# One float per run: a broadcast skip vector loaded in place, and the small loads of the start put under one semaphore

## The chip, the cores and the metric

The kernel runs on 1 core of one Trainium2 chip. The metric is the device time of one execution in microseconds (us), as the median of several executions. The time before is 993.97 us, the median of three (991.53 to 995.42).

## What is computed

Two layers of a decoder trunk on 256 tokens of width 1024, all in float32. Layer 0 mixes with a pooling group and a Mamba-2 group, layer 1 with a Conformer convolution and a gated short convolution. Every layer then cross-attends into 256 memory tokens and applies a squared-ReLU MLP. Cut to what the change touches:

```
h   = rmsnorm(x, g[0]);  u = h @ w_in                     # layer 0: ab_w_in, 1024 x 3088
pool_u, z, xbc, dt_raw = split(u)
pool_out = (window_mean(pool_u) - pool_u) @ pool_w[g]     # four groups; pool_w is 4 x 128 x 128
xbc = silu(causal_dwconv(xbc, conv_w) + conv_b)
dt  = softplus(dt_raw + dt_bias);  a = -exp(a_log)        # 16 heads
y   = ssd_chunked(xs, dt, a, B, C) + d_skip[head] * xs    # d_skip: 16 floats, one for each head of 64 channels
x   = x + rmsnorm(concat(pool_out, gated_norm(y)) @ w_out, g[1])
x   = x + rmsnorm(cross_attn(rmsnorm(x, g[2]), mem, ...), g[3])   # mem: 256 x 1024
x   = x + rmsnorm(mlp(rmsnorm(x, g[4])), g[5])
```

## The kernel before

Activations are kept transposed: a tile has channels on the 128 partitions and the 256 tokens along the row, so 1024 channels are eight such tiles (`J` = 8). To keep float32 precision every matmul operand is split into a rounded high part and a low part, and a product is three matmuls: high x high, high weight x low activation, low weight x high activation (`three`, L496 to L498).

**Weights come in units.** A unit is 256 rows x 512 columns (512 KB), two tiles of 128 rows. `weight_plan` lists 284 of them in the order in which they are used. SyncE issues one DMA for each into one of six slots of `raw` (L469). ScalarE rounds it into `w_hi` (L919). VectorE (L1263) or GpSimd (L1891) subtracts to make `w_lo`. TensorE then runs 24 matmuls on it (two tiles x four column blocks x three). From unit 6 on the DMA waits until TensorE has finished the unit that held the slot.

**Each engine's order is written out by hand**, and an engine does its instructions in that order. SyncE at the start: `x` into `xtok`, units 0 to 3, then `later_inputs` (eleven small loads into `stage`, `wdt` and the vectors), units 4 and 5, then `mem_inputs` (L459 `poolw`, L460 `memtok`), and then unit 6, the first that waits. `wdt` is the 16 columns of `ab_w_in` that give dt; `dtb`, `expA` and `dall` are 16-float vectors repeated on all 128 partitions.

**ScalarE at the start**: for each of the eight h tiles, `round_to(j // 2 + 1)` and then the scaled high part `h_hi` (L937). So h tiles 6 and 7 stand behind the rounding of unit 4. After them come the two sums of squares (L948), the copy of the norm factor's row into `Rrow` (L951), `expA` (L954), unit 5 (L919) and the copy of the vectors (L965).

**VectorE at the start**: the low parts `h_lo` (L1274), `w_lo` of unit 4, the mean square (L1295), a wait for four loads on `ssm_landed`, two copies (L1300) that pick the even and the odd heads out of `dall` for the lower and the upper 64 partitions of `dskip`, eight small multiplies that make `wdtg` (L1303), and then the first projected tiles (L1309), which need `Rrow`. The depthwise convolution (L1329, L1332) follows.

**GpSimd** makes the norm factor from the mean square by a power (L1914), and TensorE spreads it into a row after unit 3 (L577, the matmuls that `Rrow` copies). TensorE needs h tile 6 for the first matmul of unit 3, waits for `poolw` only after the SSD part, and for `memtok` after the second group of projections.

`dskip` is read once, in `gate_y`, as a per-partition scalar.

Of the kernel before, what the change touches and what calls it, by code (L numbers as in the profile page):

```python
# [38 lines left out]
P = 128  # L39
SLOTS = 6  # L40
# [4 lines left out]
class Ledger:  # L45
# [5 lines left out]
    def tick(self, sem, *label):  # L51
        self.count[sem] = self.count.get(sem, 0) + 1
        if label:
            assert (sem, *label) not in self.at, label
            self.at[(sem, *label)] = self.count[sem]
        return 1

    def after(self, sem, *label):
        if self.known is None:
            return 1  # L60
        return self.known[(sem, *label)]
# [168 lines left out]
def trunk(nc, A, out, known):  # L230
    T = A["x"].shape[1]
    D = A["x"].shape[2]
    J = D // P
    HEADS = A["ssm_a_log"].shape[1]
# [4 lines left out]
    tick, after, now = L.tick, L.after, L.now  # L239
# [39 lines left out]
    with ctx:  # L279
        def sb(name, shape, dt=F32, scope=ctx):  # L280
            return scope.enter_context(nc.sbuf_tensor(name, [P, *shape], dt))

        def sem(name):
            return ctx.enter_context(nc.semaphore(name))
# [31 lines left out]
        with ExitStack() as s:  # L316
            xdt = sb("xdt", [TT, D], scope=s)
            mp_hi, mp_lo = sb("mp_hi", [4, T], F32R, s), sb("mp_lo", [4, T], F32R, s)
            E = sb("E", [4, 3 * P], scope=s)
            cbm = sb("cbm", [2, 3 * P], scope=s)  # L320
            zs = sb("zs", [J, T], scope=s)
            xc = sb("xc", [12, T], scope=s)
            upad = sb("upad", [2, 2, T + 3], scope=s)
            pu = sb("pu", [4, T + 16], scope=s)
            pw1, pw2 = sb("pw1", [T + 16], scope=s), sb("pw2", [T + 16], scope=s)
            pdiff = sb("pdiff", [4, T], scope=s)
            Sg = sb("Sg", [2, T], scope=s)
            Rg = sb("Rg", [2, T], scope=s)
            icnt = sb("icnt", [4, 16], scope=s)
            poolw = sb("poolw", [4, P], scope=s)  # L330
            wdt, wdtg = sb("wdt", [J, HEADS], scope=s), sb("wdtg", [J, HEADS], scope=s)
            dtT = sb("dtT", [T], scope=s)
            dtb, expA, dskip = sb("dtb", [HEADS], scope=s), sb("expA", [HEADS], scope=s), sb("dskip", [J], scope=s)
            dall = sb("dall", [HEADS], scope=s)
            sp = sb("sp", [10, 2 * HEADS], scope=s)
            cs = sb("cs", [4, HEADS], scope=s)
        with ExitStack() as s:
# [11 lines left out]
        with ExitStack() as s:  # L349
# [4 lines left out]
        ps = ctx.enter_context(nc.psum_tensor("ps", [P, 8, 512], F32))  # L354


        x_landed, gain_landed, mem_landed, vec_landed, ssm_landed, poolw_landed, out_stored = (
            sem(n) for n in ("x_landed", "gain_landed", "mem_landed", "vec_landed", "ssm_landed", "poolw_landed",
                             "out_stored"))
        raw_landed = [sem(f"raw_landed{i}") for i in range(SLOTS)]  # L360
        hi_ready, lo_ready_dve, lo_ready_pool = (sem(n) for n in ("hi_ready", "lo_ready_dve", "lo_ready_pool"))

        pe_made, act_made, dve_made, pool_made = sem("pe_made"), sem("act_made"), sem("dve_made"), sem("pool_made")
# [15 lines left out]
        misc_at, n = {}, 0  # L379
# [17 lines left out]
        def bank2(label):  # L397
            return ps[:, use[label][0], :].rearrange("p (c t) -> p c t", c=2)

        def full(label):  # L400
            return pe_made, after("pe", label)

        def freed(engine, label):
            L.at[("free", label)] = (engine, now(engine))
# [37 lines left out]
        @block.sync  # L442
        def _(sp_):
            sp_.dma_start(xtok[:, :, :], A["x"][0].rearrange("(t p) d -> p t d", p=P)).then_inc(x_landed, 16)

            def later_inputs():
                for name, v in MISC_ROWS:
                    r0 = misc_at[name] - MISC
                    sp_.dma_start(stage[r0:r0 + v.shape[0], 1, :], v).then_inc(vec_landed, 16)
                sp_.dma_start(stage[:, 2, :], dw_rows[0:P, :]).then_inc(vec_landed, 16)  # L450
                sp_.dma_start(stage[0:DWN - P, 3, :], dw_rows[P:DWN, :]).then_inc(vec_landed, 16)
                sp_.dma_start(wdt[:, :, :], A["ab_w_in"][0, :, 3072:3088].rearrange("(j p) h -> p j h", p=P))\
                    .then_inc(ssm_landed, 16)
                sp_.dma_start(dtb[:, :], A["ssm_dt_bias"].broadcast_to([P, HEADS])).then_inc(ssm_landed, 16)
                sp_.dma_start(expA[:, :], A["ssm_a_log"].broadcast_to([P, HEADS])).then_inc(ssm_landed, 16)
                sp_.dma_start(dall[:, :], A["ssm_d"].broadcast_to([P, HEADS])).then_inc(ssm_landed, 16)

            def mem_inputs():
                sp_.dma_start(poolw[:, :, :], A["pool_w"][0].rearrange("g i o -> i g o")).then_inc(poolw_landed, 16)  # L459
                sp_.dma_start(memtok[:, :, :], A["mem"][0].rearrange("(t p) d -> p t d", p=P)).then_inc(mem_landed, 16)  # L460

            for u in range(NU):
                if u == 4:
                    later_inputs()
                if u == SLOTS:
                    mem_inputs()
                if u >= SLOTS:
                    sp_.wait_ge(pe_made, after("pe", "unit", u - SLOTS))
                sp_.dma_start(raw[:, u % SLOTS, :, :], units[u]).then_inc(raw_landed[u % SLOTS], 16)  # L469
            for i in range(4):  # L470
                hf, t = i // 2, i % 2
                sp_.wait_ge(dve_made, after("dve", "otok", i))
                sp_.dma_start(out[0, t * P:(t + 1) * P, hf * 512:(hf + 1) * 512],
                              otok[:, t, hf * 512:(hf + 1) * 512]).then_inc(out_stored, 16)
            sp_.wait_ge(out_stored, 16 * 2 * TT)
# [3 lines left out]
        def _(pe):  # L479
# [189 lines left out]
            for i in range(8):  # L669
                g = i // 4  # L670
# [13 lines left out]
                if i >= 2:  # L684
                    y_pair(i - 2)

            pe.wait_ge(poolw_landed, 16)
            for i in range(2):
                acquire(("pooled", i))
                for c in range(2):  # L690
                    g = 2 * i + c
# [219 lines left out]
        def _(act):  # L911
# [38 lines left out]
            act.wait_ge(*full(("R0",)))  # L950
            nc.scalar.activation(Rrow[:, :], bank(("R0",))[:, 0:T], ACT.Copy).then_inc(act_made, tick("act", "Rrow", 0))  # L951
            freed("act", ("R0",))
            act.wait_ge(ssm_landed, 16 * 4)
            nc.scalar.activation(expA[:, :], expA[:, :], ACT.Exp).then_inc(act_made, tick("act", "expA"))  # L954

            def silu_pair(i):
# [76 lines left out]
            for i in range(2):  # L1033
                for c in range(2):
                    g = 2 * i + c
# [80 lines left out]
            for l in range(2):  # L1116
                m_out = [("out", l, g, q) for g in range(2) for q in range(2)]
                if l == 1:
# [14 lines left out]
                    for g in range(2):  # L1133
                        for q in range(2):
                            i = 2 * g + q
# [101 lines left out]
            for g in range(2):  # L1237
# [6 lines left out]
                for i in (2 * g, 2 * g + 1):  # L1244
                    for c in range(2):
                        j = 2 * i + c
# [6 lines left out]
        def _(dve):  # L1253
            V = nc.vector
# [12 lines left out]
            def own():  # L1267
                dve.wait_ge(dve_made, now("dve"))
# [24 lines left out]
            for t in range(TT):  # L1293
                dve.wait_ge(act_made, after("act", "ss0", t))
            V.tensor_scalar(stat[:, 1, 0:2], stat[:, 0, 0:2], 1.0 / D, RMS_EPS, ALU.mult, ALU.add)\  # L1295
                .then_inc(dve_made, tick("dve", "v0"))
            dve.wait_ge(ssm_landed, 16 * 4)
            dpair = dall[:, :].rearrange("p (j two) -> p j two", two=2)
            for hf in range(2):
                V.tensor_copy(dskip[64 * hf:64 * hf + 64, :], dpair[64 * hf:64 * hf + 64, :, hf])\  # L1300
                    .then_inc(dve_made, tick("dve", *(("dskip",) if hf else ())))
            for j in range(J):
                V.tensor_scalar(wdtg[:, j, :], wdt[:, j, :], gain(0, 0, j), None, ALU.mult)\  # L1303
                    .then_inc(dve_made, tick("dve", *(("wdtg",) if j == J - 1 else ())))
# [134 lines left out]
            def gate_y(i):  # L1439

                dve.wait_ge(*full(("y", i)))
                dve.wait_ge(act_made, after("act", "z", i))
                dve.wait_ge(dve_made, after("dve", "dskip"))
                if i:
                    dve.wait_ge(dve_made, after("dve", "yg", i - 1))
                for c in range(2):
                    j = 2 * i + c
                    V.scalar_tensor_tensor(out=tmp[:, c, :], in0=xc[:, j, :], scalar=dskip[:, j:j + 1],
                                           in1=bank2(("y", i))[:, c, :], op0=ALU.mult, op1=ALU.add)\
                        .then_inc(dve_made, tick("dve"))  # L1450
                freed("dve", ("y", i))
                own()
                V.tensor_tensor(zs[:, 2 * i:2 * i + 2, :], zs[:, 2 * i:2 * i + 2, :], tmp[:, :, :], ALU.mult)\
                    .then_inc(dve_made, tick("dve", "yg", i))
# [36 lines left out]
            for g in range(4):  # L1491
# [4 lines left out]
                if g % 2 == 1:  # L1496
                    freed("dve", ("pooled", g // 2))
            gate_y(2)
            gate_y(3)
            group_sum(1)  # L1500
            low_to(F_[("out", 0, "early", 1)] + 3)
# [228 lines left out]
            for l in range(2):  # L1730
                if l == 1:
# [7 lines left out]
                    for g in range(2):  # L1739
# [9 lines left out]
                        for q in range(2):  # L1749
                            i = 2 * g + q  # L1750
# [9 lines left out]
                    for g in range(2):  # L1760
# [4 lines left out]
                        for q in range(2):  # L1765
                            i = 2 * g + q
# [5 lines left out]
                            for k in range(3):  # L1772
                                own()
                                for c in range(2):
                                    j = 2 * i + c
# [11 lines left out]
                    for g in range(2):  # L1787
                        for q in range(2):
                            i = 2 * g + q
# [81 lines left out]
            for i in range(4):  # L1871
                g, t = i // 2, i % 2
# [174 lines left out]
```

## Time and profile before

| | |
|---|---|
| median of three runs | 993.97 us (991.53 to 995.42) |
| the profiled execution | 995.42 us, of which its span is 993.5 us |
| TensorE matmul busy | 926.3 us (93%) |
| VectorE busy | 668.4 us (67%) |
| ScalarE busy | 472.1 us (48%) |
| GpSimd busy | 315.3 us (32%) |
| mean granted TensorE clock | 0.974 of full speed |
| DMA | 153.74 MB, 155 GB/s on average |

The rows further down are of the profiled execution. Times count from the start of its span, so a row "17.73 1.06" began at 17.73 us and was busy for 1.06 us. A bracket at the end of a row gives how long the engine had been idle just before it and what released it. A DMA's row on SPq is the time that SyncE took to issue it; when it landed is a separate column.

### The profile page before, as it was taken

The numbers are of one execution on the slowest core, as the hardware profiler recorded it, in microseconds if no ns is written. First come the engines' busy times: TensorE is split into PE (matmuls) and PEld (weight loads), VectorE is DVE, ScalarE is ACT, GpSimd is POOL, SyncE is SP. The second block draws the span as 40 slices with busy tenths as digits, with TensorE's granted clock in tenths as the row PEclk, the third lists the DMA queues.
The fourth block names the chain that finished last, engine by engine and source line by source line (L and its number), as shares of the span: only waits on it lengthen the run. The fifth ranks groups of instructions, "written<-read, shape, count | busy, mean of one in ns | idle before, by whom it ended". The sixth has DMA issues, their size and how long they took to land.

```text
span 993.5 us, 17155 instructions
## 1 busy us (share of the span) xinstructions
PE 926.3 (93%) x7268; PEld 899.3 (91%) x7268; DVE 668.4 (67%) x1013; ACT 472.1 (48%) x660; POOL 315.3 (32%) x213
## 2 busy tenths in 40 slices
PE   5978988989999999999989998999998889999997
PEld 5878987879898999999989998889998789999996
DVE  6796497686648655455588999986586385544553
ACT  4443444454546444444454433636465364444443
POOL 3242482542324100000158877536441330000000
PEclk8998999999999999999999999999999989999999
DMA  8443532455354555665555555335542435565551
GB/s 269 136 128 99 177 107 65 148 161 159 106 170 148 190 172 174 202 186 184 188 148 170 182 180 157 100 107 169 170 149 75 138 122 175 173 198 188 186 190 44
DMA packets 81031, 153.74 MB, mean 155 GB/s; under 512 B 6251, under 2 KB 7227, under 8 KB 80955
## 3 DMA queue, kind: packets, MB, share of 16 engines
q1 hardware_dynamic: 80843, 152.60, 48.7%
q8 instruction: 57, 0.93, 0.4%
q14 instruction: 19, 0.16, 0.1%
q10 hardware_dynamic: 112, 0.05, 0.0%
HBM read 151.58 MB, written 1.05 MB: 154 GB/s over the span
## 4 chain that ended last, share of the span: by engine, by line
PE 70%; DVE 20%; ACT 3%; issue 3%; POOL 2%; DMA 1%; DVEq 0%; POOLq 0%; ACTq 0%
PE ps L496 21%; PE ps L498 21%; PE ps L497 21%; DVE ps L1618 5%; DVE w_lo L1263 3%; DVE xc L1332 2%; POOL w_lo L1891 1%; PE ps L735 1%; PE ps L737 1%; PE ps L736 1%; ACT w_hi L919 1%; DVE xc L1329 1%; PE ps L563 1%; DVE E L1480 1%; DVE cv L1781 1%
## 5 line engine op out<-in xcount | busy, mean ns | idle before, releaser
L919 ACT ACTIVATE w_hi<-raw 128x1024 fp32r<-128x1024 f32 x284 | 296.9, 1055 | 282.4 <-DMA raw<-in_mlp_w 146.7
L496 PE MATMUL ps<-h_hi,w_hi 128*128 128x256 f32 x1280 | 370.8, 290 | 30.9 <-issue 12.9
L497 PE MATMUL ps<-h_lo,w_hi 128*128 128x256 f32 x1280 | 368.1, 288 | 0.0
L498 PE MATMUL ps<-h_hi,w_lo 128*128 128x256 f32 x1280 | 367.7, 287 | 0.0
L1263 DVE TENSOR_TENSOR w_lo<-raw,w_hi 128x1024 fp32r<-128x1024 f32 x192 | 250.5, 1324 | 136.8 <-ACT w_hi L919 136.6
L1891 POOL TENSOR_TENSOR w_lo<-raw,w_hi 128x1024 fp32r<-128x1024 f32 x92 | 229.6, 2510 | 188.4 <-ACT w_hi L919 188.4
L496 PEld LDWEIGHTS ps<-h_hi,w_hi 128*128 128x128 f32 x1280 | 251.7, 197 | 35.6 <-issue 21.5
L497 PEld LDWEIGHTS ps<-h_lo,w_hi 128*128 128x128 f32 x1280 | 251.9, 197 | 0.0
L498 PEld LDWEIGHTS ps<-h_hi,w_lo 128*128 128x128 f32 x1280 | 251.7, 197 | 0.0
L1914 POOL TENSOR_TENSOR rfac<-stat,mhalf 128x2 f32<-128x2 f32 (+1 forms) x14 | 16.5, 1181 | 428.0 <-DVE stat L1548 334.3
L498 PE MATMUL ps<-r_hi,w_lo 128*128 128x256 f32 x512 | 143.8, 281 | 0.0
L496 PE MATMUL ps<-r_hi,w_hi 128*128 128x256 f32 x512 | 143.6, 280 | 0.0
L497 PE MATMUL ps<-r_lo,w_hi 128*128 128x256 f32 x512 | 142.4, 278 | 0.0
L497 PEld LDWEIGHTS ps<-r_lo,w_hi 128*128 128x128 f32 x512 | 96.3, 188 | 0.0
L496 PEld LDWEIGHTS ps<-r_hi,w_hi 128*128 128x128 f32 x512 | 96.3, 188 | 0.0
L498 PEld LDWEIGHTS ps<-r_hi,w_lo 128*128 128x128 f32 x512 | 96.1, 188 | 0.0
L1618 DVE SCALAR_TENSOR_TENSOR ps<-vpad,vecs,ps 128x256 f32<-128x256 f32 x203 | 84.5, 481 | 1.0
L1713 DVE SCALAR_TENSOR_TENSOR rsq<-ps,relu 128x512 f32<-128x512 f32 x32 | 22.0, 687 | 55.3 <-ACT relu L1107 55.3
L496 PE MATMUL ps<-mh,w_hi 128*128 128x256 f32 x128 | 37.2, 291 | 1.8 <-DVE ml L1852 1.8
L1110 ACT ACTIVATE r_hi<-rsq 128x512 fp32r<-128x512 f32 x32 | 20.2, 633 | 36.7 <-DVE rsq L1713 36.7
L496 PE MATMUL ps<-mem_hi,w_hi 128*128 128x256 f32 x128 | 37.1, 290 | 0.0
L497 PE MATMUL ps<-ml,w_hi 128*128 128x256 f32 x128 | 36.6, 286 | 0.0
(247 smaller groups left out, 1322.7 us busy)
## 6 DMA issues: line engine op xcount, KB each, us to landing
raw<-in_mlp_w SPq DMA_DIRECT2D x128, 512.0 KB, 3.8
raw<-in_cd_w_in SPq DMA_DIRECT2D x40, 512.0 KB, 3.7
raw<-in_xa_wkv SPq DMA_DIRECT2D x32, 512.0 KB, 3.8
raw<-in_ab_w_in SPq DMA_DIRECT2D x24, 512.0 KB, 3.8
raw<-in_xa_wq SPq DMA_DIRECT2D x16, 512.0 KB, 3.9
raw<-in_xa_wo SPq DMA_DIRECT2D x16, 512.0 KB, 3.8
raw<-in_cd_w_out SPq DMA_DIRECT2D x16, 512.0 KB, 3.9
raw<-in_ab_w_out SPq DMA_DIRECT2D x12, 512.0 KB, 3.7
```

The source lines that it names most:

```text
L496: nc.tensor.matmul(dst, wt[0], x[0], start=start, stop=False, skip_group_check=True)
L497: nc.tensor.matmul(dst, wt[0], x[1], start=False, stop=False, skip_group_check=True)
L498: return nc.tensor.matmul(dst, wt[1], x[0], start=False, stop=stop, skip_group_check=True)
L563: mm = nc.tensor.transpose(bank(label)[:, c:c + k], src, ident[0:k, 0:k])
L919: nc.scalar.activation(w_hi[:, v % SLOTS, :, :], raw[:, v % SLOTS, :, :], ACT.Copy)\
L1110: nc.scalar.activation(r_hi[:, h % 2, 2 * q:2 * q + 2, :], rsq[:, q, :].rearrange("p (c t) -> p c t", c=2), ACT.Copy)\
L1263: V.tensor_tensor(w_lo[:, v % SLOTS, :, :], raw[:, v % SLOTS, :, :], f(w_hi[:, v % SLOTS, :, :]), ALU.subtract).then_inc(lo_ready_dve, 1)
L1332: V.scalar_tensor_tensor(out=xc[:, j, :], in0=src, scalar=vec("convw", k * 12 + j), in1=xc[:, j, :], op0=ALU.mult, op1=ALU.add)\
L1618: V.scalar_tensor_tensor(out=acc if k < 30 else cv[:, j, :], in0=src, scalar=tap(k, j), in1=acc, op0=ALU.mult, op1=ALU.add)\
L1713: V.scalar_tensor_tensor(out=rsq[:, q, :], in0=bank(("w1", l, h, q)), scalar=0.0, in1=relu[:, q, :], op0=ALU.max, op1=ALU.mult)\
L1891: G.tensor_tensor(w_lo[:, v % SLOTS, :, :], raw[:, v % SLOTS, :, :], f(w_hi[:, v % SLOTS, :, :]), ALU.subtract).then_inc(lo_ready_pool, 1)
L1914: G.tensor_tensor(dst, src, mhalf[:, 0:dst.shape[1]], ALU.pow).then_inc(pool_made, tick("pool", *name))
```

## The change

The vector `ssm_d` is no longer loaded as `dall` and rearranged by VectorE. Two DMAs write it into `dskip` directly, one for each half of the partitions. Each takes every second of the 16 floats, eight of them, and repeats them on 64 partitions. `poolw` and `memtok` move from behind unit 5 to the end of `later_inputs`, ahead of unit 4. `poolw` now counts on `ssm_landed`. Every wait on that semaphore (VectorE before `wdtg`, ScalarE before `expA`, TensorE before the pooled matmuls) is for all six loads. The semaphore `poolw_landed`, the tile `dall`, the two copies and a wait for them in `gate_y` go away.

```diff
@@ sync engine, later_inputs
-                sp_.dma_start(dall[:, :], A["ssm_d"].broadcast_to([P, HEADS])).then_inc(ssm_landed, 16)
-
-            def mem_inputs():
-                sp_.dma_start(poolw[:, :, :], A["pool_w"][0].rearrange("g i o -> i g o")).then_inc(poolw_landed, 16)
+                for hf in range(2):
+                    sp_.dma_start(dskip[64 * hf:64 * hf + 64, :],
+                                  A["ssm_d"].rearrange("a (j two) -> a two j", two=2)[:, hf, :].broadcast_to([64, J]),
+                                  allow_slow_non_contiguous=True).then_inc(ssm_landed, 16)
+                sp_.dma_start(poolw[:, :, :], A["pool_w"][0].rearrange("g i o -> i g o")).then_inc(ssm_landed, 16)
                 sp_.dma_start(memtok[:, :, :], A["mem"][0].rearrange("(t p) d -> p t d", p=P)).then_inc(mem_landed, 16)
             for u in range(NU):
                 if u == 4:
                     later_inputs()
-                if u == SLOTS:
-                    mem_inputs()
@@ tensor engine
-            pe.wait_ge(poolw_landed, 16)
+            pe.wait_ge(ssm_landed, 16 * 6)
@@ scalar engine
-            act.wait_ge(ssm_landed, 16 * 4)
+            act.wait_ge(ssm_landed, 16 * 6)
@@ vector engine
-            dve.wait_ge(ssm_landed, 16 * 4)
-            dpair = dall[:, :].rearrange("p (j two) -> p j two", two=2)
-            for hf in range(2):
-                V.tensor_copy(dskip[64 * hf:64 * hf + 64, :], dpair[64 * hf:64 * hf + 64, :, hf])\
-                    .then_inc(dve_made, tick("dve", *(("dskip",) if hf else ())))
+            dve.wait_ge(ssm_landed, 16 * 6)
@@ gate_y
-                dve.wait_ge(dve_made, after("dve", "dskip"))
```

On SyncE's queue, from `wdt` to the first unit that waits, before (a row names the line, the tile written, the tensor read and the shape):

```order
L452 DMA wdt<-in_ab_w_in 128x8x16
L454 DMA dtb<-in_ssm_dt_bias 128x16
L455 DMA expA<-in_ssm_a_log 128x16
L456 DMA dall<-in_ssm_d 128x16
L469 DMA raw<-in_ab_w_in 128x2x512 x2
L459 DMA poolw<-in_pool_w 128x4x128
L460 DMA memtok<-in_mem 128x2x1024
L469 DMA raw<-in_ab_w_in 128x2x512 [waits pe_made] x18
```

and the same stretch with the change (line numbers from here on are up to three lower above `gate_y`):

```order
L450 DMA wdt<-in_ab_w_in 128x8x16
L452 DMA dtb<-in_ssm_dt_bias 128x16
L453 DMA expA<-in_ssm_a_log 128x16
L455 DMA dskip<-in_ssm_d 64x8x1 x2
L458 DMA poolw<-in_pool_w 128x4x128
L459 DMA memtok<-in_mem 128x2x1024
L466 DMA raw<-in_ab_w_in 128x2x512 x2
L466 DMA raw<-in_ab_w_in 128x2x512 [waits pe_made] x18
```

Units 4 and 5 (the pair `x2`) now stand last of the loads that wait for nothing, behind one more small DMA, the pooling weights and the memory tokens.

On VectorE, around the end of the first projection, before:

```order
L1263 TENSOR_TENSOR w_lo<-raw,w_hi 128x1024 [waits hi_ready]
L1295 TENSOR_SCALAR stat<-stat 128x2 [waits act_made]
L1300 COPY dskip<-dall 64x8 [waits ssm_landed]
L1300 COPY dskip<-dall 64x8
L1303 TENSOR_SCALAR wdtg<-wdt,vecs 128x16 x8
L1309 TENSOR_TENSOR upad<-ps,Rrow 128x2x256 [waits pe_made,act_made]
```

and with the change:

```order
L1260 TENSOR_TENSOR w_lo<-raw,w_hi 128x1024 [waits hi_ready]
L1292 TENSOR_SCALAR stat<-stat 128x2 [waits act_made]
L1296 TENSOR_SCALAR wdtg<-wdt,vecs 128x16 [waits ssm_landed]
L1296 TENSOR_SCALAR wdtg<-wdt,vecs 128x16 x7
L1302 TENSOR_TENSOR upad<-ps,Rrow 128x2x256 [waits pe_made,act_made]
```

The two copies are gone, and the wait on the small loads sits on the first multiply of `wdtg`.

## Rows read from the trace of the kernel before

**Rows 1.** Page: busy time; then the chain that ended last, share by engine.
```profile
PE 926.3 (93%) x7268; PEld 899.3 (91%) x7268; DVE 668.4 (67%) x1013; ACT 472.1 (48%) x660; POOL 315.3 (32%) x213
...
PE 70%; DVE 20%; ACT 3%; issue 3%; POOL 2%; DMA 1%; DVEq 0%; POOLq 0%; ACTq 0%
```

**Rows 2.** The chain around 28 us: start, length, engine, tile, line.
```profile
27.97 0.12 PE ps L498
28.09 0.46 PE ps L577 x4
28.55 0.02 issue
28.57 0.38 ACT Rrow L951
28.95 0.10 ACT expA L954
29.06 0.94 ACT w_hi L919
30.00 0.44 ACT vecs L965 x2
30.44 0.03 issue
30.46 2.12 DVE xc L1329
```

**Rows 3.** SyncE's queue, timeline: issue start, issue time, line, transfer.
```profile
7.65 0.40 SPq L452 DMA_DIRECT2D wdt<-in_ab_w_in  x1
8.09 1.67 SPq L454 DMA_DIRECT2D dtb<-in_ssm_dt_bias  x1
9.81 0.55 SPq L455 DMA_DIRECT2D expA<-in_ssm_a_log  x1
10.40 0.63 SPq L456 DMA_DIRECT2D dall<-in_ssm_d  x1
11.07 0.94 SPq L469 DMA_DIRECT2D raw<-in_ab_w_in  x2
12.06 0.90 SPq L459 DMA_DIRECT2D poolw<-in_pool_w  x1
13.00 1.10 SPq L460 DMA_DIRECT2D memtok<-in_mem  x1
```

**Rows 4.** DMA issues, 0 to 80 us: size, us from issue to landing.
```profile
memtok<-in_mem SPq DMA_DIRECT2D x1, 1024.0 KB, 9.5
poolw<-in_pool_w SPq DMA_DIRECT2D x1, 256.0 KB, 7.9
...
wdt<-in_ab_w_in SPq DMA_DIRECT2D x1, 64.0 KB, 5.4
...
dtb<-in_ssm_dt_bias SPq DMA_DIRECT2D x1, 8.0 KB, 5.9
expA<-in_ssm_a_log SPq DMA_DIRECT2D x1, 8.0 KB, 5.7
dall<-in_ssm_d SPq DMA_DIRECT2D x1, 8.0 KB, 5.9
```

**Rows 5.** Units 4, 5 and 6, issued from 10 to 20 us: landing min/median/max.
```profile
DMA to landing us min/median/max: 4.3/6.6/7.6
```

**Rows 6.** DMA packets from 11 to 12 us, and from 13 to 15 us.
```profile
DMA packets 1268, 0.16 MB, mean 156 GB/s; under 512 B 1094, under 2 KB 1268, under 8 KB 1268
...
DMA packets 158, 0.01 MB, mean 5 GB/s; under 512 B 158, under 2 KB 158, under 8 KB 158
```

**Rows 7.** Stretches: PE, PEld, DVE, ACT, POOL busy (instructions), PEclk, DMA share, GB/s.
```profile
11.00:12.00 1.00, 0.00 (x0) 0.00 (x0) 1.00 (x1) 1.00 (x3) 1.00 (x1) 1.00 1.38 156
...
13.00:14.00 1.00, 0.00 (x0) 0.00 (x1) 1.00 (x3) 1.00 (x3) 0.54 (x1) 0.50 0.03 4
14.00:15.00 1.00, 0.97 (x4) 1.00 (x5) 1.00 (x1) 0.19 (x1) 1.00 (x1) 0.50 0.05 6
...
16.00:17.00 1.00, 1.00 (x7) 1.00 (x6) 1.00 (x3) 0.00 (x0) 0.11 (x1) 0.50 1.06 410
```

**Rows 8.** ScalarE, timeline: start, busy, line, operation, idle before.
```profile
17.73 1.06 ACT L919 ACTIVATE w_hi<-raw 128x1024 fp32r<-128x1024 f32 x1 [3.54 <-DMA raw<-in_ab_w_in]
18.69 0.89 ACT L937 ACTIVATE h_hi<-xT,vecs 128x256 fp32r<-128x256 f32 x2
```

**Rows 9.** VectorE, timeline, 18 to 29 us.
```profile
18.24 1.86 DVE L1274 SCALAR_TENSOR_TENSOR h_lo<-xT,vecs,h_hi 128x256 fp32r<-128x256 f32 x4
...
21.91 0.17 DVE L1295 TENSOR_SCALAR stat<-stat 128x2 f32<-128x2 f32 x1 [0.67 <-ACT sq L948]
21.99 0.39 DVE L1300 COPY dskip<-dall 64x8 f32<-64x8 f32 x2
22.41 1.47 DVE L1303 TENSOR_SCALAR wdtg<-wdt,vecs 128x16 f32<-128x16 f32 x8
28.99 1.29 DVE L1309 TENSOR_TENSOR upad<-ps,Rrow 128x512 f32<-128x512 f32 x2 [5.12 <-ACT Rrow L951]
```

**Rows 10.** GpSimd's power and TensorE's R0, timeline.
```profile
22.16 0.72 POOL L1914 TENSOR_TENSOR rfac<-stat,mhalf 128x2 f32<-128x2 f32 x1 [6.05 <-DVE dskip L1300]
...
27.93 0.60 PE L577 MATMUL ps<-ident,rfac 128*128 128x128 f32 x4
```

**Rows 11.** TensorE, timeline: its first projection matmul, and unit 3's first.
```profile
14.03 0.55 PE L496 MATMUL ps<-h_hi,w_hi 128*128 128x256 f32 x1 [4.51 <-DVE h_lo L1274]
...
25.05 0.28 PE L496 MATMUL ps<-h_hi,w_hi 128*128 128x256 f32 x1
```

**Rows 12.** The chain: one matmul's step near 16 us, and one near 22 us.
```profile
16.07 0.21 PE ps L498
...
21.97 0.12 PE ps L496
```

More of the change, by code:

```diff
@@ L333, in trunk @@
             dtb, expA, dskip = sb("dtb", [HEADS], scope=s), sb("expA", [HEADS], scope=s), sb("dskip", [J], scope=s)
-            dall = sb("dall", [HEADS], scope=s)
             sp = sb("sp", [10, 2 * HEADS], scope=s)
@@ L354, in trunk @@
         ps = ctx.enter_context(nc.psum_tensor("ps", [P, 8, 512], F32))
-        x_landed, gain_landed, mem_landed, vec_landed, ssm_landed, poolw_landed, out_stored = (
-            sem(n) for n in ("x_landed", "gain_landed", "mem_landed", "vec_landed", "ssm_landed", "poolw_landed",
-                             "out_stored"))
+        x_landed, gain_landed, mem_landed, vec_landed, ssm_landed, out_stored = (
+            sem(n) for n in ("x_landed", "gain_landed", "mem_landed", "vec_landed", "ssm_landed", "out_stored"))
         raw_landed = [sem(f"raw_landed{i}") for i in range(SLOTS)]
```

## The prediction

> **What bounds the kernel now.** The page first: TensorE is busy for 93% of the span and holds 70% of the chain that ended last [rows 1], so over the whole run the kernel is bound by TensorE. The change touches only the first 30 us, and there the chain decides. It runs through TensorE's first four weight units to the matmuls that spread the norm factor (28.09), then through the copy into Rrow, expA, unit 5's rounding and the copy of the vectors to VectorE's convolution at 30.46 [rows 2]. Whatever makes that passage late makes all behind it late, since the convolution needs Rrow and VectorE's stream from there is on the chain. So two questions count: what does the change put ahead of that passage, and how much slack does each thing ahead of it have?
>
> **What is removed.** Two copies of 0.39 us together [rows 9] and two waits. Behind them VectorE sits idle for 5.12 us until Rrow comes [rows 9], and GpSimd's power needs the mean square, which stands ahead of the copies. Taking the copies away is worth nothing. One small DMA (dall) goes too, and is priced below with what takes its place.
>
> **What is moved: poolw and memtok, ahead of units 4 and 5.** SyncE's queue gave its loads in the order wdt, dtb, expA, dall, unit 4, unit 5, poolw, memtok [rows 3]. From issue and time to landing [rows 3, 4], wdt landed at 7.65 + 5.4 = 13.05, dtb at 8.09 + 5.9 = 14.0, expA at 9.81 + 5.7 = 15.5, dall at 10.40 + 5.9 = 16.3, poolw at 12.06 + 7.9 = 19.96 and memtok at 13.00 + 9.5 = 22.5. Units 4 and 5 took 6.6 and 7.6 us, while unit 6 took the 4.3 [rows 5]. Unit 4 thus landed at 17.7, where ScalarE had been waiting for it for 3.54 us [rows 8]. Unit 5, issued half of 0.94 us later, landed at 11.54 + 7.6 = 19.1. Landings come in the order of issue, and from 16 us the transfers run at 410 GB/s [rows 7]: the DMA engines are full. The distance from unit 5's landing to memtok's, 22.5 - 19.1 = 3.4 us, is what poolw and memtok take. With the change unit 4 is later by that, and nothing hides it on the DMA side. SyncE's own issue time isn't the limit: its issue of unit 4 moves from 11.07 to about 15 (two of dskip at 0.6 to 1.7 us each, then 0.90 and 1.10 [rows 3]), and with unit 6's 4.3 us it would land at 19.4, ahead of its turn.
>
> **What is added: dskip by two DMAs.** Its source steps over every second float, so no run is longer than one float. Each DMA has 64 x 8 = 512 runs, 1024 for both, where dall had 128. No row shows a run of one float, so I bound its price from both sides.
> Low end: wdt has 128 x 8 = 1024 runs of 64 bytes from 1024 different places, and 1094 packets under 512 bytes went through in the one microsecond from 11 to 12 [rows 6]. By that 1024 runs cost 1.0 us.
> High end: dtb, expA and dall are 128 runs each, and all runs of one read the same 64 bytes. They landed 0.95, 1.5 and 0.8 us apart. From 13 to 15 us only 158 packets went through and the DMA engines were 3 to 5% busy [rows 6, 7], while unit 4 had been issued at 11.07 and stood waiting behind them. By the three together, (16.3 - 13.05) / 384 = 8.5 ns for a run, so 1024 runs are 8.7 us; by the quickest of the three (0.8 / 128) they are 6.4 us, by the slowest (1.5 / 128) 12 us.
> Which end? What sets wdt apart from the three is neither the size of a run (64 bytes in all) nor the count (wdt has eight times as many). It is that the three read one place over and over. dskip does that too: all its 1024 reads fall into the same 64 bytes. The engines were idle during it, so it is not the work of moving packets. A load behind was already queued, so it is hardly the issuing either. I take 8.7 us. Against dall's 0.8 us this is 7.9 us more. A gain is excluded, since eight times as many runs read the same place.
>
> The Trainium skill, "DMA: Bandwidth & Descriptors", Rules for kernel authors, says that a strided last dimension is lowered to one descriptor per element and should be rearranged. It speaks against this change, and agrees with 1024 runs; no run here shows it yet. [...]
>
> **Where unit 4's delay goes.** Shift of its landing: 3.4 + 7.9 = 11.3 us, so it lands at 29.0. Two paths hang on it, each with slack.
> First, h tiles 6 and 7: ScalarE makes them behind unit 4's rounding. It began unit 4 at 17.73 and the two tiles at 18.69 [rows 8], VectorE finished h_lo of tile 6 about 0.46 us (a quarter of 1.86) before 20.10 [rows 9], so 2.0 us after the landing. TensorE wants it at 25.05, unit 3's first matmul [rows 11]. Slack: 25.05 - 19.7 = 5.4 us.
> Second, the norm factor: sums of squares, mean square, power, ready at 22.16 + 0.72 = 22.88 [rows 10], 5.2 us after the landing, wanted at 27.93 [rows 10]. Slack: 5.05 us.
> The first 5 us of delay are free, covered by the matmuls of units 0 to 2. A shift of 11.3 makes R0 late by 11.3 - 5.05 = 6.2 us over the second path. Over the first, unit 3 starts at 29.0 + 2.0 = 31.0, 5.9 us late, after TensorE has stood idle for 5.9 us. At the start it stood idle for 4.5 us and the granted clock then was 0.50, the 1.2 GHz level, from 13 to 17 us [rows 7, 11]. A matmul's step was 0.21 us there and 0.12 us at full clock [rows 12]. Unit 3's 24 matmuls at the low level take 5.0 us and not 2.9, 2.2 us more. R0 is then late by 5.9 + 2.2 = 8.1 us, and that is later than the second path's 6.2.
>
> **Who else waits.** VectorE's wait for six loads instead of four is met when poolw lands: 15.5 + 8.7 + (19.96 - 19.1) = 25.1, while the mean square ahead of it on VectorE (21.91 [rows 9]) now comes 11.3 later, about 33.2. It costs nothing. The eight multiplies for wdtg (1.47 us) then end at about 35, a microsecond ahead of R0. ScalarE's wait before expA comes behind R0, TensorE's for poolw much later. Unit 5, wanted at 29.06, lands 1.4 us behind unit 4, still ahead of R0. Memtok arrives sooner, but nothing wants it before TensorE gets through its second projection.
>
> **The sum.** Copies 0; VectorE's longer wait 0; poolw and memtok 3.4 us and dskip 7.9 us of delay to unit 4; less 5.4 us of slack to unit 3; plus 2.2 us (rounded from 24 x 0.09) of low clock: 8.1 us on the path. The profiled execution (995.42 us, span 993.5) would be 1003.5 us; it was the slowest of the three runs, so against the median of 993.97 the forecast is 1002.1 us. Without the low clock it is 1000.2 (by the second path). With the bounds of a run's price: at 6.4 us both together give 5.9 us, at 12 us 11.5 us, so 999.9 to 1005.5.
>
> **Rivals.**
> *The delay fits into the slack.* If runs of one float cost what wdt's do (1.0 us), unit 4 shifts by 3.4 + 0.2 = 3.6 us, less than 5.05, and nothing moves: 994.0 us. It decides as long as both dskip DMAs together stay under 0.8 + 5.05 - 3.4 = 2.5 us. For it speaks that wdt's 1024 short runs passed quickly; against it, that wdt doesn't read one place.
> *Half way.* Reads of one place are slow, but only until the three vectors share the memory's attention, or four bytes are quicker than 64: 2.5 to 6 us for both. TensorE then stands idle for up to 3 us and may keep its clock: 0 to 3.5 us, 994 to 997.5.
> *Dearer than any row.* Writing four bytes into a partition at a time costs on top. Above 12 us for both, 1005.5 us and more.
> *A gain.* The DMA stream gets denser behind unit 5, so unit 6 on might land earlier; but those units are gated by TensorE's progress and not by SyncE, and no row shows them late here. More than 5 us of it isn't in these 30 us.
>
> **How the numbers follow.** The forecast case has 0.55, the slack case 0.24, half way 0.13, dearer 0.05, a gain 0.03. The likeliest case's own range is 999.9 to 1005.5. Since the slack case may not be left out, the range for 8 in 10 is 993.0 to 1006.0; what is left out are the dearer case, the gain, and some runs of the slack case below 993. About 0.5% (5 us) is what a measurement of this kernel can tell from no change. Slower by more than that: 0.55 + 0.05, less 0.02 for its low edge, 0.58. Within it: 0.24 + 0.13 + 0.02 = 0.39. Faster: 0.03.
>
> **What would show it.** In the profile after: dskip's landings 8 to 9 us behind expA's at 15.5; ScalarE idle before unit 4 for some 15 us instead of 3.54; TensorE idle ahead of unit 3 for about 6 us, for h_lo; clock at 0.50 and steps of 0.21 behind that; R0 near 36; and from there a timeline that is the old one, moved. If dskip lands within 3 us of expA, the price of a run is wrong and the slack case holds. If R0 is near 34 at full clock, only the clock term is wrong. If all this shows and the end is not late, then something behind 30 us takes the delay up, and the claim that the passage passes it on one to one is wrong.

## The result: 10 us slower, nearly all of it by the first convolution

The changed kernel takes 1004.97 us as the median of four runs (1001.53 to 1009.68), beside 994.69 us for the kernel before in four (991.53 to 998.91). The ratio that goes with this measurement is 1.0126, with a 95% interval of 1.0083 to 1.0169. It fits the median of all 39 executions of the changed kernel taken for it (1006.8 us, 1001.25 to 1014.23) better than that of the first four, which alone would give 1.010. In a later comparison, with ten runs against thirty-one, it is 1.0095 (1.0065 to 1.0126). Executions more than 1.5% above the quickest of the same kernel are left out of every ratio. So the change costs about 1%, some 9 to 12 us; the forecast was 8.1.

The profiled execution has a span of 1003.3 us, 9.8 more than the 993.5 before. Its page shows the same matmuls (compare [rows 1]), and in the row PEclk, the granted clock of TensorE in tenths of full speed over 40 slices of the span, a slice near the start at 7, which the kernel before does not have (8998 at its start):

```profile
span 1003.3 us, 17151 instructions
PE 929.2 (93%) x7268; PEld 902.0 (90%) x7268; DVE 668.2 (67%) x1011; ACT 471.7 (47%) x660; POOL 315.0 (31%) x213
PEclk8897999999999999999999999999999989999999
```

**SyncE's queue and the landings.** The same views as [rows 3] and [rows 4], start and time of each issue, and then size and us from issue to landing:

```profile
9.75 0.55 SPq L453 DMA_DIRECT2D expA<-in_ssm_a_log  x1
10.34 1.40 SPq L455 DMA_DIRECT2D dskip<-in_ssm_d  x2
11.78 0.62 SPq L458 DMA_DIRECT2D poolw<-in_pool_w  x1
12.45 3.71 SPq L459 DMA_DIRECT2D memtok<-in_mem  x1
16.20 21.25 SPq L466 DMA_DIRECT2D raw<-in_ab_w_in  x6
```
```profile
memtok<-in_mem SPq DMA_DIRECT2D x1, 1024.0 KB, 16.2
poolw<-in_pool_w SPq DMA_DIRECT2D x1, 256.0 KB, 14.3
...
expA<-in_ssm_a_log SPq DMA_DIRECT2D x1, 8.0 KB, 4.4
```

The view of the tile dskip gives the landing times of its two DMAs one by one, shortest, median and longest:

```profile
DMA to landing us min/median/max: 8.2/10.7/13.2
```

The second of them began to be issued at 11.10 (the row of the chain below), so dskip was complete at 24.3. expA had landed at 9.75 + 4.4 = 14.15, so the two DMAs held the queue for 10.15 us. Each float is a packet of its own: the page counts 7163 packets under 512 bytes, 6251 before, and the 912 more are near the 1024 of dskip less the 128 of dall. From 14 to 20 us hardly anything but these floats passes, at a twentieth of the engines' time or less:

```profile
DMA packets 639, 0.00 MB, mean 0 GB/s; under 512 B 639, under 2 KB 639, under 8 KB 639
...
q1 hardware_dynamic: 639, 0.00, 4.7%
```

That is 107 packets a microsecond, 9.4 ns each (10.15 us over all 1024 make 9.9). Behind dskip come poolw at 11.78 + 14.3 = 26.1 and memtok at 12.45 + 16.2 = 28.65, and then unit 4.

**The path.** The chain that ended last now begins in SyncE's queue and waits for unit 4 (start, length, what; compare [rows 2]):

```profile
11.10 0.64 SPq L455
...
16.20 13.79 DMA raw<-in_ab_w_in
30.01 1.06 ACT w_hi L916
31.06 0.41 ACT h_hi L934
31.50 0.49 DVE h_lo L1271
...
36.10 0.21 PE ps L495
...
37.05 0.46 PE ps L574 x4
37.53 0.38 ACT Rrow L948
38.02 0.94 ACT w_hi L916
38.96 0.44 ACT vecs L962 x2
39.42 2.45 DVE xc L1322 x2
```

Unit 4 is rounded at 30.01 instead of 17.73. The matmuls of R0 start 8.96 us later than before (37.05 against 28.09), and so does the first convolution (39.42 against 30.46). The timelines of ScalarE, VectorE and TensorE show who waited (start, busy, operation, idle before; compare [rows 8, 9, 11]):

```profile
30.01 1.06 ACT L916 ACTIVATE w_hi<-raw 128x1024 fp32r<-128x1024 f32 x1 [15.89 <-DMA raw<-in_ab_w_in]
```
```profile
31.50 0.88 DVE L1271 SCALAR_TENSOR_TENSOR h_lo<-xT,vecs,h_hi 128x256 fp32r<-128x256 f32 x2 [12.45 <-ACT h_hi L934]
```
```profile
32.13 0.55 PE L493 MATMUL ps<-h_hi,w_hi 128*128 128x256 f32 x1 [7.02 <-DVE h_lo L1271]
```

And the granted clock (in the column before the DMA share) fell to its lower level, 0.50, after TensorE had been idle, and unit 3 ran at it:

```profile
26.00:28.00 2.00, 0.00 (x0) 0.00 (x0) 0.00 (x0) 0.00 (x0) 0.00 (x0) 1.00 1.03 407
28.00:30.00 2.00, 0.00 (x0) 0.00 (x0) 0.00 (x0) 0.00 (x0) 0.00 (x0) 0.85 1.04 386
30.00:32.00 2.00, 0.00 (x0) 0.00 (x0) 0.50 (x2) 1.99 (x4) 0.00 (x0) 0.50 1.05 386
32.00:34.00 2.00, 1.87 (x9) 1.91 (x10) 1.51 (x2) 1.97 (x4) 0.00 (x0) 0.50 0.80 295
```

**Behind the convolution.** The delay is not quite constant from there on. TensorE's transposes of memtok begin at 54.4 us, before at 45.5, which is 8.9 later. The first product with dskip begins at 150.4, before at 140.4: 10.0 later. A part of the difference is clock. At two stretches that match but for the shift of 9 us, first the kernel before, then the changed one, TensorE was already at full clock in the one and not yet in the other, and it issued 19 matmuls against 15:

```profile
74.00:76.00 2.00, 2.00 (x19) 2.00 (x18) 1.93 (x5) 0.68 (x2) 0.00 (x0) 1.00 0.00 0
```
```profile
83.00:85.00 2.00, 2.00 (x15) 2.00 (x14) 1.93 (x6) 0.00 (x0) 0.00 (x0) 0.74 0.00 0
```

### The profile page after: what moved, and what is told of

The parts are those of the page before. It is cut to its first block, busy times and chain, and to the rows that moved or that the text cites. A ratio compares the mean times of both kernels' runs of the same rounds, so it can differ in the third digit from the quotient of the medians.

```text
span 1003.3 us, 17151 instructions
## 1 busy us (share of the span) xinstructions
PE 929.2 (93%) x7268; PEld 902.0 (90%) x7268; DVE 668.2 (67%) x1011; ACT 471.7 (47%) x660; POOL 315.0 (31%) x213
## 2 busy tenths in 40 slices
DMA packets 81943, 153.74 MB, mean 153 GB/s; under 512 B 7163, under 2 KB 8139, under 8 KB 81867
## 4 chain that ended last, share of the span: by engine, by line
PE 69%; DVE 19%; ACT 3%; issue 3%; POOL 2%; DMA 2%; SPq 1%; DVEq 0%; POOLq 0%; ACTq 0%
PE ps L493 21%; PE ps L495 20%; PE ps L494 20%; DVE ps L1610 5%; DVE w_lo L1260 2%; DVE xc L1325 2%; POOL w_lo L1883 1%; DMA raw<-in_ab_w_in 1%; ACT w_hi L916 1%; PE ps L732 1%; PE ps L734 1%; PE ps L733 1%; DVE xc L1322 1%; DVE E L1472 1%; DVE cv L1773 1%
## 5 line engine op out<-in xcount | busy, mean ns | idle before, releaser
L493 PE MATMUL ps<-r_hi,w_hi 128*128 128x256 f32 x512 | 143.6, 280 | 0.0
```

The lines of the kernel that those rows point to most:

```text
L493: nc.tensor.matmul(dst, wt[0], x[0], start=start, stop=False, skip_group_check=True)
```

## The experiments

The theory had four parts: reads of one place are slow one by one, the move of poolw and memtok alone fits into the slack, the delay acts through what stands behind unit 4 on ScalarE, and the rest of the kernel passes the delay on. Ratios below are to the kernel before on the same chip, with 95% intervals, from 10 to 12 runs of each changed kernel and 23 to 35 of the one before.

### The move alone

```diff
             (the kernel before)
-            def mem_inputs():
                 sp_.dma_start(poolw ...)      # now the end of later_inputs, behind dall
                 sp_.dma_start(memtok ...)
...
-                if u == SLOTS:
-                    mem_inputs()
```

> The kernel before with one part of the change: poolw and memtok go ahead of units 4 and 5; dall and the two copies stay. Theory (slack): unit 4 lands 3.4 us later than before, about 21.1 us, which is less than the 5.05 us of slack, so the first convolution still begins near 30.5 and the time is that of the kernel before, within 1 us. Rival (the order of the loads is what costs): the first convolution is late by 3 us or more, some 998 us.

Measured: 1.0018 (0.9986 to 1.005). Unit 4 is rounded at 21.77, a shift of 4.0 us, and R0 is on time:

```profile
21.77 1.06 ACT L915 ACTIVATE w_hi<-raw 128x1024 fp32r<-128x1024 f32 x1 [7.62 <-DMA raw<-in_ab_w_in]
...
28.69 0.38 ACT L947 ACTIVATE Rrow<-ps 128x256 f32<-128x256 f32 x1 [2.84 <-PE ps L573]
```

Rrow is copied at 28.69, before at 28.57. The idle time of ScalarE went from one place to the other (3.54 and 6.77 us before, 7.62 and 2.84 now). The slack holds. The move by itself costs nothing at R0, and nothing in the time that these runs can tell from zero (the interval reaches from -1.4 to 5 us).

### dskip alone

```diff
             (the changed kernel)
-                sp_.dma_start(poolw[:, :, :], ...).then_inc(ssm_landed, 16)
-                sp_.dma_start(memtok[:, :, :], ...).then_inc(mem_landed, 16)
+            def mem_inputs():                  # behind unit 5 again
+                sp_.dma_start(poolw[:, :, :], ...).then_inc(poolw_landed, 16)
+                sp_.dma_start(memtok[:, :, :], ...).then_inc(mem_landed, 16)
```

> The change without the move: dskip by its two DMAs, but poolw and memtok behind unit 5 as before, with a semaphore of their own for poolw. Theory: dskip lands near 24.3 as in the kernel after, unit 4 lands 1.4 us behind it at 25.7 to 26.4, a shift of 8.0 to 8.7 us; TensorE stands idle ahead of unit 3 for some 3 us; the first convolution is 3 us late at full clock and 5 us at the low one, so 997.5 to 1000 us. Rival (the move and dskip cost only together, or dskip is cheap): no change from before.

Measured: 1.0068 (1.0037 to 1.01), median 1002.43 us. Every wait on `ssm_landed` is for five loads here. Unit 4 is rounded at 25.60, a shift of 7.9 us, and TensorE waits ahead of unit 3:

```profile
27.72 0.35 PE L498 MATMUL ps<-h_hi,w_hi 128*128 128x256 f32 x1 [2.98 <-DVE h_lo L1276]
```

R0's matmuls are at 32.32, 4.2 us late, between the 3 and the 5 that were expected, since the lower clock set in only while unit 3 was running. The time is above the range expected (6.8 us by the ratio, 4.2 of them at R0); the rest is not located. So the parts don't add up: the move alone costs nothing, dskip alone 4.2 us at R0, both together 8.96. The slack is spent once, and what comes on top of it is paid: the move adds 4.4 us to unit 4's shift (12.3 against 7.9) and 4.7 us to the delay at R0.

### One float from 128 places

```diff
-                                  A["ssm_d"].rearrange("a (j two) -> a two j", two=2)[:, hf, :].broadcast_to([64, J]),
+                                  A["x"][0][64 * hf:64 * hf + 64, 0:16].rearrange("p (j two) -> p two j", two=2)[:, 0, :],
```

> The whole change, but the two DMAs of dskip read from x, each partition its own row (eight floats, every second one, rows 4 KB apart), so there are again 1024 runs of one float, from 128 places. dskip then holds numbers of x and not the skip vector. Theory (reading one place over and over is what is slow): the two DMAs take 1 to 2 us in all, unit 4 lands near 21 to 22, and the time is that of the kernel before within 1 us. Rival (a run of one float is what is slow, wherever it is read): dskip takes 10 us as in the kernel after, unit 4 lands at 30, some 1005 us.

Measured: 1.0006 (0.9979 to 1.0034). The same 1024 runs of one float, but each partition has its own row:

```profile
dskip<-in_x SPq DMA_DIRECT2D x2, 2.0 KB, 4.7
...
expA<-in_ssm_a_log SPq DMA_DIRECT2D x1, 8.0 KB, 4.3
```
```profile
DMA to landing us min/median/max: 4.2/4.7/5.3
```

expA landed at 9.85 + 4.3 = 14.15. The second DMA of dskip, issued at about 11.2, landed by 16.5: 2.4 us for both, not 10.15. Unit 4 is rounded at 21.26 and R0 is on time. The rival, that a one-float run is dear wherever it is read, is out. dskip holds numbers of x here and in the next experiment, so these two kernels leave out the skip vector and compute something else; only their times count.

### One float from sixteen places, read 64 times each

```diff
-                                  A["ssm_d"].rearrange("a (j two) -> a two j", two=2)[:, hf, :].broadcast_to([64, J]),
+                                  A["x"][0][0:1, 512 * hf:512 * hf + 512].rearrange("a (j k) -> a k j", k=64)[:, 0, :]
+                                  .broadcast_to([64, J]),
```

> The whole change, but the two DMAs of dskip read one float from each of eight places 256 bytes apart (a row of x), the same eight for all 64 partitions, so 1024 runs of one float from sixteen places in all, each read 64 times. dskip holds numbers of x. Theory in its narrow form (it is the single place that serves one read at a time): eight places side by side are quicker, 1.5 to 4 us for both, and the first convolution is on time or up to 1 us late, 995 to 997 us. Wide form (all reads of a neighbourhood of a few KB get in each other's way): still 9 to 10 us, some 1005 us.

Measured: 0.9983 (0.9948 to 1.0018).

```profile
dskip<-in_x SPq DMA_DIRECT2D x2, 2.0 KB, 3.8
...
expA<-in_ssm_a_log SPq DMA_DIRECT2D x1, 8.0 KB, 4.1
```

expA landed at 13.73, poolw, behind dskip, at 11.68 + 3.7 = 15.4, and unit 4 was rounded at 20.88. Both DMAs together took 1.7 us at most. All 64 partitions still read the same places, only eight of them side by side and 256 bytes apart. The narrow form of the theory holds: what is slow is the single place, not the neighbourhood and not the broadcast as such. One gap is left: both quick sources lie in x, and no run read a single place of x, so that the small vectors' own location plays a part isn't excluded. Against it stands that dtb, expA and dall, three tensors, were all slow in the kernel before.

### 64 bytes at a time from the one place

```diff
-                    sp_.dma_start(dskip[64 * hf:64 * hf + 64, :],
-                                  A["ssm_d"].rearrange(...)[:, hf, :].broadcast_to([64, J]), ...)
+                    sp_.dma_start(dmany[64 * hf:64 * hf + 64, :, :],          # 64 x 8 runs of all 16 floats
+                                  A["ssm_d"].unsqueeze(1).broadcast_to([64, J, HEADS])).then_inc(ssm_landed, 16)
```

> The whole change, but each of the two DMAs moves 512 runs of 64 bytes (all 16 floats of ssm_d, eight times for each partition) and the two copies pick dskip out of them. 1024 runs again, all reading the one place, sixteen times as long. Theory (a read of the one place has its price whatever its length): 8.5 to 10 ns a run as for dtb, expA and dall, 9 to 10 us for both, and the time is that of the kernel after, 1003 to 1007 us. Rival (four-byte writes or reads have a price of their own): clearly under 8 us for both DMAs.

Measured: 1.0104 (1.0068 to 1.014), median 1005.46 us.

```profile
dmany<-in_ssm_d SPq DMA_DIRECT2D x2, 32.0 KB, 10.7
```
```profile
DMA to landing us min/median/max: 8.2/10.7/13.3
```
```profile
DMA packets 639, 0.04 MB, mean 7 GB/s; under 512 B 639, under 2 KB 639, under 8 KB 639
```

Sixteen times the bytes, and the same two landing times within 0.1 us, and 639 packets from 14 to 20 us as before. A read of the one place costs 9 to 10 ns for 4 bytes as for 64. Four bytes have no price of their own.

### The slow DMAs put last

```diff
             (dskip alone, as above)
-            (the two DMAs of dskip at the end of later_inputs)
             def mem_inputs():
                 sp_.dma_start(poolw ...)
                 sp_.dma_start(memtok ...)
+                for hf in range(2):
+                    sp_.dma_start(dskip[64 * hf:64 * hf + 64, :], ...).then_inc(skip_landed, 16)
...
             (gate_y)
+                dve.wait_ge(skip_landed, 16 * 2)
```

> dskip still by its two DMAs, but issued last of the loads that wait for nothing, behind unit 5, poolw and memtok, on a semaphore of their own that only the gating of y waits for. Theory: they still take 10 us, but units 4 and 5 land as before (17.7 and 19.1), so the first convolution is on time; unit 6, issued at 19.5, lands behind dskip at about 33 to 34, where ScalarE asks for it at 33.03: 0 to 1 us late, so 994 to 996 us. Rival (short runs slow every transfer down, wherever they stand): units 4 and 5 are late as well, and the time is over 998 us.

Measured: 0.9999 (0.9971 to 1.0027).

```profile
memtok<-in_mem SPq DMA_DIRECT2D x1, 1024.0 KB, 9.6
...
dskip<-in_ssm_d SPq DMA_DIRECT2D x2, 2.0 KB, 13.9
```
```profile
13.04 2.46 SPq L460 DMA_DIRECT2D dskip<-in_ssm_d  x2
```
```profile
16.82 1.06 ACT L921 ACTIVATE w_hi<-raw 128x1024 fp32r<-128x1024 f32 x1 [2.71 <-DMA raw<-in_ab_w_in]
```

memtok lands at 21.6. dskip's second DMA, issued at 13.8, took 16.1 us and landed at about 29.9, 8.4 us behind memtok. So the slow reads are still there, nearly in full. Unit 4 comes even sooner than before, and unit 6 was there when ScalarE got to it at 32.24: no wait at all. The expectation had it land at 33 to 34 and be up to 1 us late. Repeated beside the last experiment:

> The kernel with the two dskip DMAs issued last, again, beside the one above. Expected 0.997 to 1.003 of the kernel before, as the first time, since its 9 us on the DMA queue end before unit 6 is asked for by more than 1 us.

Measured: 1.0008 (0.9977 to 1.0038).

### Unit 4 taken out of the way

```diff
             for j in range(J):
-                round_to(j // 2 + 1)
+                round_to(min(j // 2 + 1, 3))
                 h_part("in0", 0, 0, j)
...
                 (behind the two sums of squares)
+            round_to(4)
...
                 (VectorE: low part of unit 4 behind wdtg)
-                    low_to(j // 2 + 1)
+                    low_to(min(j // 2 + 1, 3))
...
+            low_to(4)
```

> The whole change, with ScalarE's and VectorE's order turned so that unit 4 stands behind h tiles 6 and 7, the sums of squares, the mean square and wdtg (and still ahead of Rrow). Unit 4 lands at 30.0 as in the kernel after. Theory (the delay acts only through what stands behind unit 4 on ScalarE): R0 is on time near 28, Rrow is copied when unit 4 has been rounded, at about 31.1, and VectorE makes the low part of unit 4 at 31 to 32.3 ahead of the convolution's input; the first convolution begins 3 to 3.5 us later than before and not 9 us; TensorE doesn't wait ahead of unit 3. Some 998 us. Rival (the late DMA queue itself holds up more than this): the time stays near that of the kernel after, over 1003 us.

Measured: 1.0066 (1.0032 to 1.01), median 1002.35 us. Unit 4 is rounded at 29.98, as late as in the changed kernel, but R0's matmuls stand at 27.23 in TensorE's timeline (before 27.93, changed kernel 36.9). ScalarE and VectorE:

```profile
29.98 1.06 ACT L916 ACTIVATE w_hi<-raw 128x1024 fp32r<-128x1024 f32 x1 [12.98 <-DMA raw<-in_ab_w_in]
30.94 0.37 ACT L949 ACTIVATE Rrow<-ps 128x256 f32<-128x256 f32 x1
```
```profile
31.06 1.23 DVE L1261 TENSOR_TENSOR w_lo<-raw,w_hi 128x1024 fp32r<-128x1024 f32 x1 [3.99 <-ACT w_hi L916]
32.20 1.28 DVE L1304 TENSOR_TENSOR upad<-ps,Rrow 128x512 f32<-128x512 f32 x2
33.60 1.70 DVE L1324 TENSOR_SCALAR xc<-upad,vecs 128x256 f32<-128x256 f32 x2
```

The first convolution begins at 33.60, 3.1 us late and not 9: two thirds of the delay at this place hung on the order on ScalarE, as the theory has it. The time, though, is not the 998 us expected: its median lies nearer to the rival's 1003 us, and only the lower end of the interval (3.2 us) agrees with 3.1. Its interval also overlaps that of the changed kernel, so the time alone doesn't decide between theory and rival; the rows do, for this place. TensorE now waited 3.29 us for expA and then ran the dt matmuls in 5.30 us at the lower clock, which the expectation left out:

```profile
31.45 5.30 PE L605 MATMUL ps<-xT,wdtg 128*16 128x256 f32 x16 [3.29 <-ACT expA L952]
```

In the kernel before they took 3.61 us. Its own profiled execution was a quick one (span 995.2), and its first product with dskip came at 143.6, 3.2 us later than before. What the other 2 to 3.5 us of the time are is open.

### The changed kernel again

> The changed kernel itself again, beside the others on one chip. By the shift of the first convolution read from its profile (9.0 us) the ratio to the kernel before is 1.009; the earlier 1.0126 would want another 3 us from behind 40 us. Theory: 1.009 to 1.011, the rest being the granted clock's stretches, which differ from execution to execution. Rival: again 1.0126 or above, so something behind the start adds to it.

Measured: 1.0095 (1.0065 to 1.0126). In its profile R0 is copied at 37.56, 8.99 us later than before. The transposes of memtok begin at 54.5 (9.0 later than before) and the first product with dskip at 151.1 (10.7 later), so this execution too loses more behind the convolution. The start accounts for 9.0 us, the ratio for 9.5 with an interval of 6.5 to 12.6. It doesn't refute the 12.5 of the first measurement, whose interval (8.3 to 16.9) holds 9.5 as well: the rival is less likely, and not excluded.

### A kernel that might beat both

The chain shows expA and unit 5's rounding on the passage, though ScalarE idled for 6.77 us ahead of it.

```diff
             (the kernel before)
+            act.wait_ge(ssm_landed, 16 * 4)
+            nc.scalar.activation(expA[:, :], expA[:, :], ACT.Exp) ...
+            round_to(first[("xbc", 0)] + 5)
             act.wait_ge(*full(("R0",)))
             nc.scalar.activation(Rrow ...)
-            act.wait_ge(ssm_landed, 16 * 4)
-            nc.scalar.activation(expA[:, :], expA[:, :], ACT.Exp) ...
```

> The kernel before, with two of ScalarE's instructions taken out of the passage at 28 us and put into its idle time ahead of it: the exponential of expA and the rounding of unit 5 (landed at 19.1) now stand ahead of the copy into Rrow. Theory: the copy of the vectors, and with it the first convolution, comes 1.0 us earlier after R0 (0.10 and 0.94 us leave the chain), and the span is shorter by that; 1 us of 995 is inside the interval, so the ratio is 0.999 with 1 in it. Rival: the vectors' matmuls or Rrow's reader on VectorE take the place of it, and the convolution moves by less than 0.3 us.

Measured: 1.003 (0.9996 to 1.0064). The rival was right. The copy of the vectors came 1.2 us earlier, 1.0 of it behind R0, but VectorE's first two products, which need only Rrow, took its place:

```profile
28.79 1.29 DVE L1310 TENSOR_TENSOR upad<-ps,Rrow 128x512 f32<-128x512 f32 x2 [5.91 <-ACT Rrow L954]
30.18 0.73 DVE L1330 TENSOR_SCALAR xc<-upad,vecs 128x256 f32<-128x256 f32 x2
```

From R0 to the convolution it is 2.29 us instead of 2.37. No kernel tried here is shown to beat the one before.

## Why the prediction was right, and where its size was short

**Which runs cost what.** Right. It said 8.7 us for dskip's two DMAs because dtb, expA and dall were slow and wdt wasn't, and named reading one place as the difference. The three experiments on the source confirm it: 128 places 2.4 us, sixteen places 1.7 us at most, one place with 64-byte runs 10 us. The size was low: 10.15 us, 9.9 ns a run and not 8.5. It didn't show in the landing, because expA landed at 14.15 and not at 15.5. dskip was forecast to land at 24.2 and landed at 24.3: two errors of 1.4 us that cancel, which is luck. Why expA came sooner is open; dall isn't it, since with the move alone, where dall still stands behind expA, it landed at 14.35. There dall took 2.2 us and expA 0.7, where the kernel before had 0.8 and 1.5. So the price of one such vector scatters, and only the sum of the three carries (3.25 us before, 3.5 with the move alone); the bounds of 6.4 and 12 us, each from one vector, rested on that scatter. By the prediction's own sum they give 5.8 and 11.4 us, not 5.9 and 11.5.

**What poolw and memtok take.** Mis-sized: 3.4 us was expected for the two, and they took 4.35, since poolw took 1.8 us instead of 0.86. memtok's 2.55 and unit 4's 1.35 were as forecast. The 1024 KB and 256 KB were priced from a stretch in which the engines were full. Here poolw followed right behind slow reads that left the engines nearly idle, and with the move alone, where it stands behind dall, it took 1.3 us. That it pays for the engines' filling up again is argued, not shown. So unit 4 came at 30.0, not 29.0.

**The slack.** Right: 5.4 and 5.05 us. The move alone (4.0 us of shift) left R0 where it was, and dskip alone (7.9) made TensorE wait for 2.98 us. The slack case, a rival with 0.24, would have needed dskip under 2.5 us; with another source it holds, with this one not.

**The lower clock.** Right. TensorE idled for 7.02 us, the granted clock was 0.50 from 30 to 34 us, a matmul's step 0.21 until 36.3, and unit 3 took from 32.13 to 37.05, 4.9 us (forecast 5.0; before 3.0). With dskip alone the idle time was 3 us, and the lower clock came in part.

**Who else waits.** Right: VectorE's wait for six loads ended with poolw at 26.1, well ahead of the mean square at 34.19. wdtg was done before R0.

**The sum.** 8.1 us was forecast for the first convolution and 8.96 was measured. Unit 3 began 7.1 us late and not 5.9, most of the difference being poolw's; the low clock cost 1.9 us and not 2.2. Applied to the median before, 8.96 gives 1002.9 us, inside the range.

**What failed.** The first measurement's ratio of 1.0126 stands for 12.5 us on 993.97, 1006.5 us, which is past the 1006.0 of the range; the second stands for 9.5 us. Two steps of the prediction were wrong. The first is the term of 3.4 us for poolw and memtok, which measured 4.35; it makes the delay at R0 0.9 us larger. The second is the step from the convolution to the end, "a timeline that is the old one, moved": it was put at nothing, and in the profiles the delay grew from 9.0 us at 60 us to 10.0 and 10.7 at the first product with dskip, in part because TensorE ran longer at 0.50 behind 77 us. Over the 39 executions of the changed kernel the mean granted clock is 0.968, over 35 of the kernel before 0.974. On 1000 us that difference is 6 us of clock, of which unit 3's stretch at 0.50, some 7 us long, makes 3.4. The other 2.5 could cost TensorE up to 2.5 us in stretches that differ from execution to execution. That is an estimate from these figures, and no experiment here holds the clock fixed. With it the sum would be 9 to 11.5 us. Where the rest of the 12.5 comes from, if it is there at all, stays open. The range left nothing for either step: its upper end, 1006.0, lay 0.5 us above the forecast case's own 1005.5.

## What to carry to other kernels

Count the reads of one place, not the bytes or the runs. Sixteen floats repeated on 128 partitions are cheap to look at and cost about 1 us of a DMA queue; eight floats of them picked out one by one for each partition cost ten, and everything queued behind pays. If such a load can't be avoided, issue it last and wait for it where it is used: the same DMAs, moved, cost nothing measurable here. And before a load is put ahead of a weight, ask what stands behind that weight on the engine that takes it: here it was not the weight that was missed but the activations and the norm factor in the queue behind it. Slack ahead of a passage is spent once, so two edits that each look free or cheap may not be so together. And a delay at the start need not arrive at the end unchanged: leave room for it in the range.

## What the runs showed of the hardware

- A DMA that reads one place in HBM (16 floats, 64 bytes) over and over goes at 9 to 10 ns a read, for 4 bytes as for 64, while the DMA engines show 5% busy. Eight places 256 bytes apart for each DMA, with as many reads in all, have none of it (1.7 us for 1024 reads at most). Whether the reads are held up one by one at the memory, or in each DMA engine, no run here tells apart.
- While it lasts, the issues behind it take longer: memtok's took 3.71 us against 1.10 before, and poolw's took 6.27 us with dskip alone against 0.90. A long issue time here was the cost of the DMA ahead.
- A VectorE operation beside GpSimd's w_lo can take several times as long: in the kernel before, the first two products of the convolution took 2.44 us while GpSimd made unit 5's low part (30.08 to 32.43), and 0.73 us in the last experiment, where GpSimd had done it from 23.43 on. TensorE's transposes of memtok then came 0.8 us earlier than before (44.7 against 45.5), 0.2 of it already there at R0, but the first product with dskip came 0.5 us later (140.9 against 140.4). Where the gain went isn't shown.
